# Two transformer layers written out, with steps moved across the seam between them

## The reference, cut to what matters

```
def trunk_layer(x, cond, attend, p, w_router, router_bias):
    mod = silu(cond) @ p['w_ada'] + p['b_ada']           # six vectors of 1024: "modulation"
    sh1, sc1, g1, sh2, sc2, g2 = split(mod, 6)
    h = rms_norm(x, p['norm1']) * (1 + sc1) + sh1
    q, k, v, u, gates = split(h @ p['w_in'])
    attn = attend(q, k, v) @ p['w_attn_proj']            # 8 heads, 2 key heads, window 128, sink
    conv = conv_module(u) @ p['w_conv_proj']             # GLU, depthwise conv 31, layer norm, swish
    x = x + g1 * ((sigmoid(gates_a) * attn + sigmoid(gates_c) * conv) @ p['w_out'])
    h = rms_norm(x, p['norm2']) * (1 + sc2) + sh2
    x = x + g2 * moe(h)                                  # 16 experts of 512, 1 of 4 groups, top 2
    return x, k, v

for l in range(2): ...                                   # both token groups through layer l
y_prompt, y_sample = rms_norm(xp, final_norm), rms_norm(xs, final_norm)
```

## Time and profile before

| | us |
|---|---|
| median of three runs | 1303.47 (1302.17 to 1304.31) |
| profiled execution, own time | 1307.92 |
| its span, first to last instruction | 1306.3 |
| TensorE busy in the span | 1141.0 (87%) |
| VectorE busy | 733.6 (56%) |
| ScalarE busy | 493.8 (38%) |
| mean granted TensorE clock | 0.936 of full speed |

### The profile page before, as it was taken

One profiled execution on the slowest core, in us unless ns is written; L12 is line 12 of the kernel. 1 busy time (PEld: TensorE's weight loads), 2 busy tenths in 40 slices (PEclk: granted clock), 3 DMA queues, 4 the chain that ended last, 5 costly groups with the idle time before them and its releaser, 6 DMA issues.

```text
span 1306.3 us, 21238 instructions
## 1 busy us (share of the span) xinstructions
PE 1141.0 (87%) x6452; PEld 788.3 (60%) x6453; DVE 733.6 (56%) x1448; ACT 493.8 (38%) x803; POOL 9.2 (1%) x27
## 2 busy tenths in 40 slices
PE   4899989997679999999689998999859879999983
PEld 2698767687454455554359876768836445455543
DVE  2577988765712245444456799886472234234455
ACT  2444756532332233332153465654232222223323
POOL 0000000000000000000000000000000000000000
PEclk8899989998789999999789999999969989999996
DMA  7733655325456899999583273552352889889941
GB/s 296 249 101 132 256 182 206 129 71 189 168 188 229 313 368 394 394 395 394 230 287 101 97 282 138 210 178 67 132 228 96 311 300 395 316 317 396 394 178 49
DMA packets 140910, 305.59 MB, mean 234 GB/s; under 512 B 7136, under 2 KB 47824, under 8 KB 134672
## 3 DMA queue, kind: packets, MB, share of 16 engines
q1 hardware_dynamic: 138160, 301.62, 63.6%
q10 hardware_dynamic: 2528, 2.50, 0.6%
q0 software_dynamic: 128, 0.26, 0.1%
HBM read 302.53 MB, written 1.84 MB: 233 GB/s over the span
## 4 chain that ended last, share of the span: by engine, by line
PE 64%; DVE 18%; issue 11%; ACT 3%; DMA 3%; DVEq 1%; ACTq 0%; SPq 0%
PE ps L615 15%; PE ps L648 10%; PE ps L618 6%; PE ps L737 5%; PE ps L774 4%; PE ps L775 4%; PE ps L776 4%; DVE conv L1598 4%; PE ps L939 3%; PE ps L673 3%; PE ps L674 2%; PE ps L751 2%; DMA rbias<-in_router_bias 2%; DVE st L1637 1%; PE ps L891 1%
## 5 line engine op out<-in xcount | busy, mean ns | idle before, releaser
L1482 DVE SCALAR_TENSOR_TENSOR nat<-ps,weight,nat 128x512 f32<-128x512 f32 x192 | 132.2, 745 | 132.2 <-PE ps L674 132.2
L1598 DVE SCALAR_TENSOR_TENSOR conv<-ub,dw,conv 128x414 f32<-128x414 f32 x240 | 137.2, 645 | 0.8
L776 PE MATMUL ps<-h_hi,w_lo 128*128 128x384 f32 x384 | 130.0, 339 | 0.0
L615 PE MATMUL ps<-ring,xgT 128*64 128x256 f32 x896 | 106.2, 390 | 4.8 <-issue 4.8
L1469 DVE TENSOR_TENSOR orow_lo<-ps,orow_hi 64x512 fp32r<-64x512 f32 (+1 forms) x64 | 44.1, 689 | 114.9 <-ACT orow_hi L1096 114.1
L615 PE MATMUL ps<-second,xgT 128*64 128x256 f32 x832 | 97.3, 386 | 8.7 <-issue 6.4
L615 PEld LDWEIGHTS ps<-ring,xgT 128*64 128x64 f32 x896 | 69.7, 140 | 43.1 <-issue 18.9
L774 PE MATMUL ps<-h_hi,gate_hi 128*128 128x384 f32 x256 | 90.3, 353 | 0.0
L615 PEld LDWEIGHTS ps<-second,xgT 128*64 128x64 f32 x832 | 62.6, 139 | 45.8 <-issue 20.1
L1082 ACT ACT_TABLE_LOAD x32 | 41.1, 1283 | 127.7 <-PE ps L615 85.5
L775 PE MATMUL ps<-h_lower,gate_hi 128*128 128x384 f32 x256 | 86.9, 339 | 0.0
(11 more groups left out here) (267 smaller groups left out, 2068.1 us busy)
## 6 DMA issues: line engine op xcount, KB each, us to landing
ring<-in_w_ada SPq DMA_DIRECT2D x48, 1024.0 KB, 7.3
ring<-in_w_e_gate SPq DMA_DIRECT2D x32, 1024.0 KB, 8.5
ring<-in_w_e_up SPq DMA_DIRECT2D x32, 1024.0 KB, 9.6
ring<-in_w_e_down SPq DMA_DIRECT2D x32, 1024.0 KB, 9.1
second<-in_w_e_gate SPq DMA_DIRECT2D x32, 1024.0 KB, 10.0
second<-in_w_e_up SPq DMA_DIRECT2D x32, 1024.0 KB, 12.2
second<-in_w_e_down SPq DMA_DIRECT2D x32, 1024.0 KB, 13.0
ring<-in_w_in SPq DMA_DIRECT2D x30, 1024.0 KB, 5.7
```

Of the source, the lines that this page charges most:

```text
L615: last = pe.matmul(ps[64 * hh:64 * hh + 64, b, 0:256], xgT[:, k, 0:64], slots[at][:, o:o + 256], start=(k == 0), stop=(k == KD - 1))
L776: last = pe.matmul(ps[:, b, 0:T], lower[:, o:o + P], hi[:, k, 0:T], start=False, stop=(k == k_tiles - 1))
L1482: dve.scalar_tensor_tensor(sums, ps[:, b, :], weight[:, t, bass.ds(at, 1)], sums, ALU.mult, ALU.add).then_inc(fr[b], 1)
L1598: dve.scalar_tensor_tensor(conv[:, i, :], src, w, conv[:, i, :], ALU.mult, ALU.add).then_inc(tapped, 1)
```

## The change

1. The layer loops of all engines are written out (`for l in range(DEPTH)`), so waits have constants. Inner loops over experts stay.
2. Start: SP loads the conditions and layer 0's parameters first, then two modulation chunks, x, and the other chunks. TensorE does the conditions and two chunks' modulation rows before it transposes x. The wait for the rotary table and the router bias moves to their first use; the caches of layer 0 are loaded at the start, those of layer 1 after the first norm.
3. Attention: `mod_cols(1)` and VectorE's `mod_out` move from the 15th filler's place to the 13th's, ahead of gate 8.
4. Routing: a sigmoid of one column into a new tile `warm` stands after the second norm on ACT. `h2n` goes through the first halves of all token tiles before the second halves; VectorE's first subtraction stands ahead of the scores, two behind the choice of experts, three behind the first half of `place`, and `spread` waits for each three where it needs them.
5. Seam: expert 15's own sums stand in its four bodies, behind its down product; before them, in layer 0, the next layer's parameters (TensorE) and its first modulation chunk, and a second chunk after the bodies. SP issues the next layer's first six chunks ahead of its `overfull` branch, and VectorE copies the parameters out after expert 15's sums. Parameters, modulation and the first sum use other banks (3, 2, 3 and 4), and the skipped second pass uses `second` and bank 5 in place of `ring` and bank 2.
6. Seam and end: `nat` is turned back by feature half, ACT squares each tile when its three token tiles are updated, and VectorE's additions stand between its updates.

```diff
-MOD2_AT = FILLERS.index(("ada2", 4)) // 2
+MOD2_AT = FILLERS.index(("gate", 8)) // 2
...
-    ("params", [7]), ("ada", [0]), ("mod", [2]), ("rms1", [3]),
+    ("params", [3]), ("ada", [2]), ("mod", [3]), ("rms1", [4]),
...
+ADA_EARLY = 2
...
+            sp.dma_start(crow[0:8, :], A["c_ctx"].rearrange("(k p) -> k p", p=P)).then_inc(c_in, 16)
...
+            sp.dma_start(prow[:, :], A["features"][0]).then_inc(par_in, 16)
+            sp.dma_start(dwrow[:, :], A["taps"][0]).then_inc(par_in, 16)
...
+            for l in range(DEPTH):
+                for c in range(0 if l == 0 else SLOTS, NCHUNKS):
+                    load_chunk(c, l)
+                    if l == 0 and c == 1:
+                        load_x()
...
+                if l + 1 < DEPTH:
+                    for c in range(SLOTS):
+                        load_chunk(c, l + 1)
...
+            for k in range(ADA_EARLY):
+                ada_rows(0, 0, k)
             pe.wait_ge(x_in, 48)
...
                     if kind == "gate":
+                        if q == 8:
+                            mod_cols(l, 1)
                         wide_split("gate", q, KD, 2, h_hi, lambda k: h_lower[:, k, :])
                     else:
-                        if q == 4:
-                            mod_cols(1)
                         for k in range(2):
-                            ada_rows(1 + q // 4, 2 * (q % 4) + k)
+                            ada_rows(l, 1 + q // 4, 2 * (q % 4) + k)
...
                         back_tiles(range(2, NT))
                         down(small)
+                        if last_one:
+                            if l + 1 < DEPTH:
+                                params(l + 1)
+                                ada_rows(l + 1, 0, 0)
+                            back(lambda b: expert_use(b, l, e), freed, full, small)
...
-                expert(NE - 1, NE - 2, True, NE // 2 - 1)
-                by_width(pe, NE - 1, lambda small: back(lambda b: expert_use(b, l, NE - 1), freed, full, small))
+                expert(NE - 1, NE - 2, True, NE // 2 - 1, True)
+                if l + 1 < DEPTH:
+                    for k in range(1, ADA_EARLY):
+                        ada_rows(l + 1, 0, k)
...
+                act.activation(warm[:], eps[:], ACT.Sigmoid)
...
-                for q in range(3):
-                    b, n = use("y", 3 + q, l)
-                    act.wait_ge(freed[b], n + 1)
-            squares(2 * DEPTH)
+                def layer_out(k):
+                    for t in range(NT):
+                        b, n = use("y", k // 4 * NT + t, l)
+                        act.wait_ge(freed[b], n + 1)
+                squares(2 * l + 2, layer_out)
...
-            dve.wait_ge(t_in, 32)
...
-                add_squares(l * 2)
+                if l == 0:
+                    add_squares(0)
+                    params_out(0)
...
+                lower_h(0)
                 b, n = use("logits", 0, l)
...
+                lower_h(1)
+                lower_h(2)
...
+                    if half_at == 0:
+                        for i in range(NT, 2 * NT):
+                            lower_h(i)
...
+                if l + 1 < DEPTH:
+                    params_out(l + 1)
...
                 for i in range(6):
...
-                    t, h = i // 2, i % 2
+                    t, h = i % NT, i // NT
...
                     last.then_inc(freed[b], 1)
+                    if i >= NT:
+                        add_square(2 * l + 2, i - NT + 1)
+                for k in range(4, KD):
+                    add_square(2 * l + 2, k)
```

More of the change, by code:

```diff
@@ L494, in expert_chunk @@
                 return w_d[bass.ds(w, 1), :, (j - 4) * 2:(j - 3) * 2, :].rearrange("o p k n -> p (o k) n")
[L496 to L510, removed]
-                    else:
[L512 to L525, removed]
@@ new lines, in load_chunk @@
+            def load_chunk(c, l):
+                s = c % SLOTS
+                if c < SLOTS:
+                    if c in (0, 2, 4):
+                        sp.wait_ge(half, l * HALF_PER + (HALF_FIRST - 5 + c // 2))
+                    else:
+                        b = {1: 2, 3: 3, 5: 6}[c]
+                        sp.wait_ge(full[b], l * PER[b] + (INIT[b] - 1))
+                else:
+                    wait_chunk_used(c - SLOTS, l)
+                kind, i, part = CHUNKS[c]
+                if kind == "ada":
+                    src = w_ada[bass.ds(l, 1), part, :, i * SLOT:(i + 1) * SLOT].rearrange("o p n -> p o n")
+                elif kind in ("aproj", "cproj"):
+                    w = w_ap if kind == "aproj" else w_cp
+                    src = w[bass.ds(l, 1), :, :, i * 512:(i + 1) * 512].rearrange("o p k n -> p (o k) n")
+                elif kind == "router":
+                    src = w_r
+                else:
+                    w = w_out if kind == "out" else w_in
+                    m = i + {"qkv": 0, "u": 3, "gate": 7, "out": 0}[kind]
+                    src = w[bass.ds(l, 1), :, :, m * 256:(m + 1) * 256].rearrange("o p k n -> p (o k) n")
+                load(ring[s], landed[s], src)
@@ L596, in _, with expert_parts @@
                 last.then_inc(full[b], 1)
[L597 to L602, removed]
+            def expert_parts(n_of, fr, fs, slots, landed_s, land_at, half_s, own_s, own_at, xg_s, xg_at, gate_bank=2):
                 def products(which, b, small):
@@ L654, in gate @@
                 def gate(small):
-                    products(0, 2, small)
+                    products(0, gate_bank, small)
                 def up(small):
@@ L660, in expert_parts, with back @@
                 return gate, up, turn_own, turn_hid, down
-            def back(n_of, fr, fs, small, tiles=range(NT)):
+            def back(n_of, fr, fs, small, tiles=range(NT), gate_bank=2):
                 if 0 in tiles:
@@ L682, in rms_sum @@
                 pe.matmul(ps[:, b, 0:T], ones[:], rstd[:], start=True, stop=True).then_inc(full[b], 1)
[L684 to L720, removed]
@@ new lines, in _ @@
+            for l in range(DEPTH):
+                if l == 0:
+                    for k in range(ADA_EARLY, KD - 2):
+                        ada_rows(l, 0, k)
+                    params(l)
+                    rms_sum("rms1", l, l * 2)
+                    for k in range(KD - 2, KD):
+                        ada_rows(l, 0, k)
+                else:
+                    for k in range(ADA_EARLY, KD):
+                        ada_rows(l, 0, k)
+                        if k == ADA_EARLY + 2:
+                            rms_sum("rms1", l, l * 2)
+                mod_cols(l, 0)
@@ L925, in _ @@
                 last.then_inc(full[b], 1)
[L928 to L930 removed]
                 for half_at in range(2):
                     for k in range(KD):
+                        if half_at == 0 and k % 4 == 0:
+                            for i in range(NT):
+                                b, n = use("h2n", k // 4 * NT + i, l)
+                                pe.wait_ge(freed[b], n + 1)
                         b, n = use("spread", half_at * KD + k, l)
@@ L1366, in _ @@
             pool.memset(zero16[:], 0.0).then_inc(consts2, 1)
-            with pool.Fori(0, DEPTH) as l:
+            for l in range(DEPTH):
                 pool.wait_ge(k_pre, l + 1)
@@ L1413, in _ @@
             dve.tensor_copy(before_b[:], before[:])
+            for i in range(6):
+                b, n = init_use("x", i)
+                t, h = i // 2, i % 2
+                dve.wait_ge(full[b], n + 1)
+                dve.tensor_copy(xT[:, 4 * h:4 * h + 4, t * P:(t + 1) * P],
+                                ps[:, b, :].rearrange("p (k n) -> p k n", k=4)).then_inc(freed[b], 1)
             dve.wait_ge(consts2, 5)
-            dve.wait_ge(t_in, 32)
             assert steps[0] == BASE
@@ L1496, in _, with link @@
                 dve.tensor_scalar(nsink[:], sinkb, -1.0, None, ALU.mult)
+            for l in range(DEPTH):
+                steps[0] = 0
+                def link(ins):
+                    steps[0] += 1
+                    ins.then_inc(chain, 1)
+                    dve.wait_ge(chain, l * CHAIN + (BASE + steps[0]))
                 def mod_out(stage, i, g):
```

141 lines of the change are left out of this document (86 added, 55 removed).

## The result

The changed kernel takes 1296.32 us (median of 15 runs, 1292.6 to 1301.47) where the kernel before took 1304.88 beside it (15 runs, 1302.17 to 1311.46). The ratio is 0.9931, 95% interval 0.992 to 0.9943: some 9 us faster, between 7.4 and 10.4. I had forecast 24.2 us and a range of 1267 to 1292. The sign was right, less than half of the size came, and the time lies outside the range.

A forecast was written before the change was run, and what follows sets the result against it. TensorE holds most of the chain; layer 0's expert weights stream at the DMA's limit. Start -1.8, attention -10.4, routing -7.2, seam -4.4, end +1.6, constant waits -2.0 sum to -24.2: 1303.5 to 1279.3 us, range 1267 to 1292.

The forecast's parts named there:

- The start: Up to the first projection: new load order and no early wait for the router bias, -1.8 us.
- the table load that I put ahead of the squares: At the start: ScalarE's table load no longer fits into the wait for x and adds 1.28 us.
- the second addition: At the start: second of VectorE's seven additions begins at about 26.8, where it began at 28.57.
- The attention: Both layers: modulation columns one filler earlier remove TensorE's wait and VectorE's idle times, together -10.4 us.
- The routing: Both layers: table loaded while ScalarE idles, four of six subtractions off the path, 3.6 us a layer, -7.2 us.
- the sums: Seam: expert 15's sums in its body no longer begin 3.22 us after their last operand, -3.2 us.
- the squares by tile: From first residual update to sum product: -5.9 us at the seam, -1.2 us at the end.
- The step that failed: the branches: Branch out of expert 15 now follows the sums in place of a short one: seam +4.2 us, end +2.8.
- Whatever brings the experts forward brings the whole stream forward: Layer 0's experts: weights stream restarts when expert 0 frees its slots, so gains ahead of the experts count in full.
- My rival on the loop: Expert loop no longer stays fetched: 14 branches at 2.98 us add 42 us, 1321 us; chance 5%.

The follow-up runs named there:

- the control: Changed kernel with 16 never executed TensorE instructions behind expert 0's wide body in layer 0: 1296.29 us.
- the sums out: Changed kernel with expert 15's sums taken out of its four bodies and put behind them, parameter products and modulation chunks after them: 1276.45 us.
- dead code in the old bodies: Kernel before with 150 never executed TensorE instructions in one untaken body of expert 15: 1311.5 us.
- the two single parts: Kernel before with one part each: modulation columns one filler earlier, 1297.69 us; dummy sigmoid and VectorE's six subtractions spread out, 1296.62 us.
- late pads of 144 and 256: Changed kernel with 144 or 256 never executed TensorE instructions in expert 0's narrow body of layer 1 alone: 1292.4 and 1300.36 us.
- the 144: Changed kernel with 144 never executed TensorE instructions behind expert 0's wide body in layer 0: 1274.93 us.

## Why the prediction was wrong

*Right.* The start: the first projection begins at 41.07 in this trace, but at 39.55 to 40.24 in seven of the other eight traces with the new load order (40.99 in the control), and at 41.4 to 42.3 in the four with the old: about -1.7 on the mean, as forecast; no kernel of its own tested it. The size was in part luck: x came at 18.90 and not at 17, and the table load that I put ahead of the squares came behind them (28.30). The terms that I gave add up to 26.4 for the second addition, not to 26.8; it came at 26.57. The attention: -10.4 worked out, -11.6 in the trace with the qkv stage in it, -8.6 timed alone (interval 6.4 to 10.7). The routing: -7.2 worked out, -7.5 in the stages alone, -9.8 timed (7.6 to 12.0). At the seam the sums began 0.25 us after their operand (forecast -3.2, measured -3.0), and the squares by tile gave 6.1 and 1.4 (5.9 and 1.2).

*The step that failed: the branches.* I took the dear ones as given and moved one: "that branch then follows the sums, where one of at most 1.68 us stood: +4.2" at the seam, "+2.8" at the end. The bodies with the sums in them are longer, and three dear jumps followed the sums at the seam (6.1, 5.4, 2.3), where I had put one: from VectorE's last addition to `nat` to the first transposition it took 14.0 us where it had taken 2.8, so 11.2 more, not 4.7. At the end it was 4.2 more, not 2.8. The kernels with the sums out and with dead code in the old bodies show this.

*The same step in the experts.* "Whatever brings the experts forward brings the whole stream forward" held for the two single parts. It failed for the whole, since the first pass over the loop got longer by jumps that I had left out of the sum: from expert 0's down products to expert 3's it took 77.8 us in layer 0, where it took 69.0. My rival on the loop had the mechanism and the wrong place: I let it fail on each pass, 14 times, or not at all. Later passes stay at 0.17 us a jump and even get shorter, 13.56 us for an expert where it was 13.81 (13.6 in all kernels with the layers written out, 13.8 in all others; which part of the change does it is untested); only the first pass pays. In layer 1 the sums of jumps mislead, 15.0 us against 6.8: up to expert 3's down products it takes 76.7 us where it took 77.2. One of the jumps cost nothing, as said, and the kernel before stands 2.83 us in straight code there, which the changed one doesn't:

```profile
1036.19 2.83 issue
```

The other 2.6 us of the 3.1 in the table are the shorter later passes. In layer 0 the stream takes them back.

I read the earlier trace rows as prices, and should have asked why five of those 63 jumps were dear and the others not. The Trainium skill's page "Runtime: NRT & Kernel Launch", section "Instruction fetch mechanics", which I weighed, says that code comes in blocks of 256 instructions and that a taken branch outside the blocks at hand waits for one. The runs agree (late pads of 144 and 256). I drew from it that straight code is cheap, which the stalls at 378.87 and 1036.19 qualify; that the layout of the branches left in it would be drawn anew was there to be read. With about the jumps of the kernel before, 28 us with the 144, the changed kernel takes 1275, within my range, but not by my sum: layer 1's experts give 9.3 us there, which I had at nothing.

*Open.* Exactly which jump is dear, and why the transfer starts up to 3.7 us after the jump in the dearest. Far or quickly repeated ones are dear here, but in the kernel with 144 in layer 0 two single jumps were dear that I had expected cheap (2.95 us in the first pass, 2.7 at the end).

## What to carry to other kernels

Where an engine's code has data-dependent bodies, list its branches by duration before you price an edit: those of some microseconds were waits for code here, and an edit that lengthens or moves the code deals them anew. See which of them stand beside running work, for those cost nothing. Work put into a body is copied into each variant, so what follows sits farther away; short bodies with the common work behind them are cheaper (here by 0.4%, 5 us, when both kernels had the 144 in layer 0). When a layout change moves the time, add never executed instructions as a control before you believe the edit: here they are worth 21 us. Such a pad holds for these inputs and this build alone.

## What the runs showed of the hardware

TensorE's jumps took 1.7 to 7.3 us or 0.07 to 0.43 in these kernels; in the changed one, a code transfer of 16 KB begins in each of the former. Straight code can stand for code as well: 2.96 us at 378.87, with such a transfer in it. The loop over the experts pays on its first pass only: seven transfers from 373 to 430, none from 429.9 to 632.2. A stall of 5 to 6 us costs more than itself: in the stretches around it the granted clock was 0.95 and 0.96, and the next 16 products took 8.83 us, not 7.06.
